# Where the second chunk's weights are split after a layer norm, and how the up projection begins

## The reference, cut to what matters

```python
for layer in range(DEPTH):                      # DEPTH = 2
    mix = hgrn2_mixer(h, ...) if layer == 0 else swa_sink_mixer(h, k_shared, v_shared, ...)
    h = layer_norm(ALPHA * h + mix, ln_mix_g[layer], ln_mix_b[layer])
    ff = conv_ffn(h, ffn_w_in[layer], conv_w, conv_b, ffn_w_out[layer])
    h = layer_norm(ALPHA * h + ff, ln_ffn_g[layer], ln_ffn_b[layer])
    if layer == 0:
        k_flat, v_flat = jnp.split(h @ shared_w_kv, 2, axis=-1)

def conv_ffn(h, w_in, conv_w, conv_b, w_out):
    u = causal_depthwise_conv(h @ w_in, width 3) + conv_b
    a, b = jnp.split(u, 2, axis=-1)
    return (silu(a) * b) @ w_out
```

## Time and profile before

| what | value |
|---|---|
| median of three executions | 1738.62 us |
| the profiled execution, its own time | 1736.45 us |
| its span in the profile | 1734.6 us |
| busy: TensorE, VectorE, ScalarE, GpSimd | 1567.9, 852.3, 610.4, 542.0 us |
| mean granted TensorE clock | 0.951 |

### The profile page before, as it was taken

One profiled execution on the slowest core, in us unless ns is written; L12 is line 12 of the kernel. 1 busy time (PEld: TensorE's weight loads), 2 busy tenths in 40 slices (PEclk: granted clock), 3 DMA queues, 4 the chain that ended last, 5 costly groups with the idle time before them and its releaser, 6 DMA issues.

```text
span 1734.6 us, 20912 instructions
## 1 busy us (share of the span) xinstructions
PE 1567.9 (90%) x7764; PEld 1275.2 (74%) x7764; DVE 852.3 (49%) x1271; ACT 610.4 (35%) x725; POOL 542.0 (31%) x408
## 2 busy tenths in 40 slices
PE   7999999889999899877767799999899779998778
PEld 6888887668888788665656588888788567886456
DVE  7778776366666600344462556666500555002761
ACT  3545453242222222244342332222222362334440
POOL 2000011425555534422011335555344325333002
PEclk9999999989999999988879899999999989998799
DMA  7411212212222222321010212222222313221001
GB/s 210 113 63 60 73 49 98 73 65 100 94 96 95 97 82 97 116 70 58 0 48 0 97 57 94 95 97 96 94 96 82 129 39 137 86 79 70 4 1 49
DMA packets 21702, 136.99 MB, mean 79 GB/s; under 512 B 2392, under 2 KB 4744, under 8 KB 6160
## 3 DMA queue, kind: packets, MB, share of 16 engines
q1 hardware_dynamic: 16992, 124.79, 20.2%
q10 hardware_dynamic: 4656, 11.45, 2.6%
HBM read 132.02 MB, written 4.21 MB: 79 GB/s over the span
## 4 chain that ended last, share of the span: by engine, by line
PE 75%; DVE 13%; issue 5%; DVEq 4%; ACT 2%; DMA 0%; ACTq 0%; POOL 0%; SPq 0%
PE pair L366 22%; PE pair L368 22%; PE pair L367 22%; PE pair L475 2%; DVE SMALL L1409 2%; DVE PL L1439 1%; PE pair L430 1%; PE pair L719 1%; PE pair L705 1%; DVE SY L1321 1%; DVE H L1318 1%; DVEq L1320 1%; ACT WH L833 1%; DVE PL L1561 1%; DVEq L1400 1%
## 5 line engine op out<-in xcount | busy, mean ns | idle before, releaser
L331 POOL TENSOR_TENSOR WL<-RAW,WH 128x512 fp32r<-128x512 f32 x268 | 367.2, 1403 | 494.1 <-ACT WH L833 494.1
L366 PE MATMUL pair<-AH,WH 128*128 128x512 f32 x1144 | 456.0, 399 | 44.2 <-DVE AL L1345 25.4
L367 PE MATMUL pair<-AL,WH 128*128 128x512 f32 x1144 | 450.4, 394 | 0.0
L368 PE MATMUL pair<-AH,WL 128*128 128x512 f32 x1144 | 450.2, 394 | 0.0
L833 ACT ACTIVATE WH<-RAW 128x2048 fp32r<-128x2048 f32 x115 | 220.0, 1913 | 607.8 <-PE pair L368 590.2
L340 POOL TENSOR_TENSOR WL<-RAW,WH 128x512 fp32r<-128x512 f32 x136 | 174.6, 1315 | 679.7 <-ACT WH L833 679.7
L366 PEld LDWEIGHTS pair<-AH,WH 128*128 128x128 f32 x1144 | 218.2, 191 | 93.6 <-issue 34.1
L368 PEld LDWEIGHTS pair<-AH,WL 128*128 128x128 f32 x1144 | 217.7, 190 | 46.3
L367 PEld LDWEIGHTS pair<-AL,WH 128*128 128x128 f32 x1144 | 218.2, 191 | 44.5 <-issue 0.5
L1318 DVE SCALAR_TENSOR_TENSOR H<-H,pair 128x512 f32<-128x512 f32 x32 | 21.5, 681 | 278.6 <-PE pair L368 278.6
L366 PE MATMUL pair<-GH,WH 128*128 (+1 forms) x352 | 141.2, 401 | 9.9 <-DVE CA L1372 9.9
(11 more groups left out here) (223 smaller groups left out, 2119.7 us busy)
## 6 DMA issues: line engine op xcount, KB each, us to landing
RAW<-stream SPq DMA_DIRECT2D x115, 1024.0 KB, 4.7
H<-x_t SPq DMA_DIRECT2D x2, 1024.0 KB, 7.3
bias_rows<-ROWS ACTq DMA_DIRECT2D x1, 2048.0 KB, 24.8
H<-x_t SPq DMA_DIRECT2D x1, 2048.0 KB, 7.7
BIAS<-bias_rows ACTq DMA_DIRECT2D x1, 2048.0 KB, 7.8
FBC<-forget_rows ACTq DMA_DIRECT2D x1, 2048.0 KB, 7.2
out<-H ACTq DMA_DIRECT2D x8, 256.0 KB, 2.0
MT<-mem_t ACTq DMA_DIRECT2D x1, 1024.0 KB, 5.8
```

The costliest lines, as they stand in the source:

```text
L331: pool.tensor_tensor(WL[slot][:, part], RAW[slot][:, part], WH[slot][:, part].bitcast(F32), ALU.subtract).then_inc(w_lo, 1)
L366: pe.matmul(out_, wh, xh, start=start, stop=False)
L367: pe.matmul(out_, wh, xl, start=False, stop=False)
L368: return pe.matmul(out_, wl, xh, start=False, stop=stop)
```

## The change

In ScalarE's layer norm `split_next` moves from ahead of the wait for the variance to behind the third block (m = 2) of the block loop; this holds for all four norms. In the up projection the first two chunks are no longer interleaved: the first is done whole, waiting for each block, then the second.

```diff
@@ ffn, TensorE
-                pieces = ((n_in, s0, (bk(0), bk(1))), (n_in + 1, 1 - s0, (bk(2), bk(3))))
-                for k in range(4):
-                    for n, s, banks in pieces:
-                        col_chunk(n, s, banks, AH, AL, ready=(a_ready, a_base), ks=(k,))
-                for n, s, banks in pieces:
-                    col_chunk(n, s, banks, AH, AL, ready=(a_ready, a_base), ks=range(4, 8))
+                col_chunk(n_in, s0, (bk(0), bk(1)), AH, AL, ready=(a_ready, a_base))
+                col_chunk(n_in + 1, 1 - s0, (bk(2), bk(3)), AH, AL)
@@ layer_norm, ScalarE
                     act.activation(SQ[:, m % 4], H[:, m], ACT.Square).then_inc(y_squared, 1)
-                split_next(n_last)
                 if load:
                     load()
                 act.wait_ge(var_made, idx + 1)
@@
                     else:
                         ins.then_inc(h_ready, 1)
                         squares(m - 1)
+                    if m == 2:
+                        split_next(n_last)
                 if not split:
                     squares(KB - 1)
```

## The result

The changed kernel takes 1745.67 us (median of six executions, 1743.60 to 1749.68) against 1737.97 us for six of the kernel before: ratio 1.0047, 95% interval 1.0034 to 1.0060. It is slower by 7.7 us; 7.1 was forecast. (Ratios here are estimated over all executions. They are not quotients of the two medians, and the two can differ by a microsecond.) The profiled execution is the slowest of the six, with a span of 1747.8 us, 13.2 over the span before.

The account below looks back on a forecast made before the run. TensorE was taken to bound the kernel, with VectorE's chain the path up to each block loop. 2.6 + 3.3 + 2.6 - 0.37 - 1.57 - 0.56 + 1.5 - 0.4 = +7.1 on 1738.62 gave 1745.7 us, range 1740.3 to 1752.

Parts of the forecast that it names:

- The mechanism: Block loop: GpSimd's four moved instructions each hold up one VectorE instruction, blocks come late, TensorE idles; +2.6, +3.3, +2.6 us.
- Removed: Variance of each norm: without GpSimd beside it the block loop starts 0.37, 1.57, 0.56 and 1.57 us earlier.
- Moved on ScalarE, on SyncE: Split of 1.9 us behind block 2, chunk load some 14 us later: cost nothing in norms 0 to 2.
- Lag: Blocks from block 3 on come 3.5 us later, bounds 1.8 and 4.5.
- Clock: TensorE's full clock comes only behind the gap, in blocks 3 and 4: 1.5 us, taken in one norm.
- The cover by the interleaved order: Before the change, twelve matmuls per block keep TensorE behind the blocks and hide VectorE's delays; six will not.
- No lag: Rival: GpSimd does not slow the block loop at all, only the earlier starts count; 1735.0 us, chance 0.05.
- small lag: Rival: GpSimd finds turns between VectorE's drains, blocks only 1.8 us late; 1738.5 us, chance 0.14.
- The longer half clock: Rival: gaps before blocks 2 and 3 keep TensorE at half clock for five blocks; 1757 us at the outside, chance 0.14.
- the forecast's side, slower: Whole kernel: the change makes it slower than before, chance 0.82.

Follow-up runs that it names:

- run 4: Changed kernel with GpSimd's four low parts of the second chunk made to wait for the last block's low part (norms 0 to 2): 1734.02 us, ratio 0.9980.
- run 5: Changed kernel with GpSimd making the second chunk's low part twice in norms 0 to 2: 1761.32 us, ratio 1.0134.
- run 1: Kernel before with only the new chunk order, first two chunks of the up projection not interleaved: 1737.47 us, ratio 0.9999.
- run 2: Changed kernel with the interleaved chunk order put back, so only the split is moved: 1745.24 us, ratio 1.0045.
- run 7: Repeat of the changed kernel with the interleaved chunk order put back: 1742.11 us, ratio 1.0033.
- run 3: Changed kernel with the split behind the whole block loop, in norm 3 behind the last squares: 1734.31 us, ratio 0.9982.
- run 10: Changed kernel with GpSimd's low parts behind the block loop (norms 0 to 2) and norm 3's split behind the last squares: 1734.35 us, ratio 0.9982.
- run 9: Changed kernel with the second chunk's low part in eight GpSimd instructions of 256 columns, not four of 512 (norms 0 to 2): 1744.34 us, ratio 1.0034.

## Why the prediction was right

**The mechanism** was named and is shown: run 4 takes GpSimd alone out of the loop and wins back the loss, so that the gain of the freed variance is left; run 5 doubles GpSimd's work there and the loss grows; run 1 clears the order. One reading behind it was loose: of the "two in a row" of 1.50 and 1.51 us in the earlier trace rows the second is a copy with a single source, not an instruction with two operands. It was held as long.

**Removed.** Forecast 0.37, 1.57, 0.56 and 1.57. From the copy of the mean to the first multiplication: 4.87, 6.13, 5.05 and 6.13 us before, 4.46, 4.48, 4.47 and 4.48 after: 0.41, 1.65, 0.58 and 1.65. Right.

**Moved on ScalarE, on SyncE.** Costed at nothing. Run 4 confirms it for ScalarE, and for SyncE too, since the low parts that release its loads come later still there.

**Lag.** Forecast 3.5, measured 4.16. This term was mis-sized: I took 1.43 us from start to start, from the pair in the earlier trace rows; it was 1.52 to 1.86 here (355.58, 357.27, 359.13, 360.65, 362.33 above). The two engines alternate, and GpSimd's four took 6.68 us instead of the 5.68 in the earlier trace rows; in a steady stream of both the pair took longer than in the earlier trace rows. That makes 0.7 us more in each of three norms, 2 us.

**Clock.** I took 1.5 us in one of three norms. The changed kernel's start took 27.93, 27.96, 27.95 and 28.00 us in the four up projections of two profiles. Full clock was there at the first or second matmul of block 2 in three of them and already in block 1 in the fourth, always ahead of the gap before block 3, so the lateness of block 3 covered the difference. So 0, and this error cancelled most of the lag's: 5.6 without it, 7.1 with it, 7.6 from the stages.

**Left out.** Two effects behind the stages were not foreseen: the 1.6 us that the second block gives back with norm 3's split moved, and the 2.5 us of half clock in norm 3's sums. They partly cancel too (+0.9). The total was closer than its terms, and that is luck.

**The cover by the interleaved order** was seen as what hides VectorE's delays now. Runs 2 and 7 show how much of it would have been left with a late split: mostly 1.3 of the 3.4 us, since the second chunk's low part is itself late.

**Rivals.** No lag and small lag are excluded by the rows of 1.60 to 1.77 us and the lag of 4.16. The longer half clock did not come at this size of gap, and came in run 5. The chance given to the forecast's side, slower, was borne out.

## What to carry to other kernels

An instruction moved into idle time on its own engine also moves what it releases on another one: here the rounding was free in both places, and the subtraction behind it on GpSimd cost 4 us of VectorE in a loop that TensorE waits for. Before moving a release, list the VectorE instructions that will run beside GpSimd (with two SBUF operands above all; the one SBUF copy in the earlier trace rows was held as well), count one GpSimd instruction for each GpSimd instruction released, and ask how much work the consumer has per step to cover it. The better place is where VectorE is idle: behind the last block of norms 0 to 2 (runs 3, 4 and 10, 0.2% faster than before the change). And put the fixed point of a stage behind everything that the moved work can meet: norm 3's lay too early, and showed a gain of 2.0 us in run 10 that was none.

## What was not expected of the hardware

Halving GpSimd's instruction (1.26 us at least for 512 columns) shortened each hold-up from 1.77 to 1.22 us but made eight of them, so the last block, at 4.15 us behind run 4's in the changed kernel, was still 3.75 behind it in run 9; GpSimd's eight took 9.07 us together against 6.68 for four. TensorE's sums of norm 1 take 2.5 us more in one execution than in another of the same kernel, by the clock granted after the same idle time of 3.1 us (17.8 or 20.2 us from the first addition to the mean). And a change in norm 3 decided, in twelve profiles of twelve, whether TensorE ran at full or fell to half clock after an idle time of about 2 us, some 40 us later.
